# Layer 1's first mean square by column quarters of TensorE instead of eight full-width products

## What is computed

```python
def _rmsnorm(x, g):
    xf = x.astype(F32)
    y = xf * lax.rsqrt(jnp.mean(xf * xf, axis=-1, keepdims=True) + NORM_EPS)
    return (y * g.astype(F32)).astype(x.dtype)
...
    hn = _rmsnorm(h, g_mix_pre) * valid[None, :, None].astype(h.dtype)
    u = (hn @ w_in).astype(F32)
```

## Time and profile before

| | us |
|---|---|
| median of three runs | 973.7 (973.14 to 974.08) |
| the profiled execution's own time | 972.89 |
| its span, first to last instruction | 970.5 |
| TensorE busy in the span | 958.7 |
| VectorE / ScalarE / GpSimd busy | 605.5 / 515.1 / 79.8 |
| mean granted clock of TensorE | 0.997 |

### The profile page before, as it was taken

One profiled execution on the slowest core, in us unless ns is written; L12 is line 12 of the kernel. 1 busy time (PEld: TensorE's weight loads), 2 busy tenths in 40 slices (PEclk: granted clock), 3 DMA queues, 4 the chain that ended last, 5 costly groups with the idle time before them and its releaser, 6 DMA issues.

```text
span 970.5 us, 18994 instructions
## 1 busy us (share of the span) xinstructions
PE 958.7 (99%) x7428; PEld 906.2 (93%) x7428; DVE 605.5 (62%) x933; ACT 515.1 (53%) x825; POOL 79.8 (8%) x72
## 2 busy tenths in 40 slices
PE   9999999999999999999999999999999999999998
PEld 7999988899989999999989998888999899999886
DVE  7776575367857655553467775753678566565543
ACT  6645654475375544444456447444854655454542
POOL 1000000000031222210100000000000322122000
PEclk9999999999999999999999999999999999999999
DMA  7874433446462655555545653344465545656652
GB/s 217 298 220 148 130 95 124 131 131 174 155 193 91 198 172 174 175 176 165 170 131 159 206 165 120 114 132 131 132 180 168 174 130 185 198 179 197 215 177 85
DMA packets 164299, 158.02 MB, mean 163 GB/s; under 512 B 9603, under 2 KB 157294, under 8 KB 163854
## 3 DMA queue, kind: packets, MB, share of 16 engines
q1 hardware_dynamic: 163118, 153.76, 51.4%
q10 hardware_dynamic: 928, 3.33, 0.9%
q0 software_dynamic: 192, 0.07, 0.0%
HBM read 154.98 MB, written 1.05 MB: 161 GB/s over the span
## 4 chain that ended last, share of the span: by engine, by line
PE 92%; DVE 3%; DMA 2%; ACT 2%; issue 1%; DVEq 0%; SPq 0%
PE banks L690 24%; PE banks L692 24%; PE banks L691 24%; PE banks L1081 2%; PE banks L1083 2%; PE banks L1082 2%; DMA raw<-in_ffn_w_up 1%; PE banks L740 1%; PE banks L725 1%; DMA raw<-in_w_out 1%; PE banks L722 1%; PE banks L721 1%; PE banks L670 1%; DVE lo L1564 1%; PE banks L948 1%; PE banks L946 1%
## 5 line engine op out<-in xcount | busy, mean ns | idle before, releaser
L1564 DVE TENSOR_TENSOR lo<-raw,hi 128x1024 fp32r<-128x1024 f32 (+1 forms) x287 | 348.3, 1217 | 145.5 <-ACT hi L1165 145.3
L690 PE MATMUL banks<-xh,hi 128*128 128x272 f32 (+1 forms) x1456 | 420.6, 289 | 0.1
L692 PE MATMUL banks<-xh,lo 128*128 128x272 f32 (+1 forms) x1456 | 416.2, 286 | 0.0
L691 PE MATMUL banks<-xl,hi 128*128 128x272 f32 (+1 forms) x1456 | 415.1, 285 | 0.0
L1165 ACT ACTIVATE hi<-raw 128x1024 fp32r<-128x1024 f32 (+1 forms) x287 | 300.2, 1048 | 135.4 <-PE banks L692 45.4
L690 PEld LDWEIGHTS banks<-xh,hi 128*128 128x128 f32 x1456 | 274.3, 188 | 6.0 <-issue 4.2
L692 PEld LDWEIGHTS banks<-xh,lo 128*128 128x128 f32 x1456 | 274.5, 189 | 0.0
L691 PEld LDWEIGHTS banks<-xl,hi 128*128 128x128 f32 x1456 | 274.2, 188 | 0.0
L1269 ACT ACTIVATE gates<-banks,par 128x272 f32<-128x272 f32 (+1 forms) x64 | 30.7, 480 | 98.4 <-PE banks L692 92.4
L2058 POOL TENSOR_TENSOR silu_g<-silu_g,rstd 128x272 f32<-128x272 f32 (+1 forms) x44 | 54.6, 1240 | 219.0 <-ACT silu_g L1444 219.0
L2051 POOL TENSOR_TENSOR sq<-sq 128x272 f32<-128x272 f32 (+1 forms) x18 | 21.4, 1191 | 600.2 <-ACT sq L1429 599.4
(11 more groups left out here) (291 smaller groups left out, 1445.9 us busy)
## 6 DMA issues: line engine op xcount, KB each, us to landing
raw<-in_w_in SPq DMA_DIRECT2D x54, 1024.0 KB, 5.2
raw<-in_ffn_w_gate SPq DMA_DIRECT2D x22, 1024.0 KB, 5.2
raw<-in_ffn_w_up SPq DMA_DIRECT2D x22, 1024.0 KB, 5.3
raw<-in_ffn_w_down SPq DMA_DIRECT2D x19, 1024.0 KB, 5.1
raw<-in_w_out SPq DMA_DIRECT2D x8, 1024.0 KB, 5.3
raw<-in_w_in SPq DMA_DIRECT2D x12, 512.0 KB, 4.2
raw<-in_w_branch SPq DMA_DIRECT2D x12, 512.0 KB, 5.4
raw<-in_ffn_w_down SPq DMA_DIRECT2D x4, 768.0 KB, 4.3
```

The source lines that it names most:

```text
L690: mm(dst, wh, mh, start=start, stop=False)
L691: mm(dst, wh, ml, start=False, stop=False)
L692: return mm(dst, wl, mh, start=False, stop=stop)
L1564: tt(half_of(lo, g, c), half_of(raw, g, c), half_of(hi, g, c).bitcast(F32), ALU.subtract).then_inc(lo_ready, 2 if g in G_MIX else 1)
```

## The change

In layer 1's entry the eight full-width matmuls of the mean square go. In their place:

- `quarter_sums`: eight matmuls by `denind` (32 columns, the first all ones, the others zero), in two rounds of four. In a round the four matmuls write the four 32-partition quarters of bank 5, from `sq` tiles 0 to 3 in the first round and 4 to 7, accumulated, in the second. The first round stands inside the three tiles' run behind step k = 5, the second behind its end. Rows 0, 32, 64 and 96 then hold four partial sums, the other rows zero.
- `take_quarters`: a new ScalarE copy of that bank into `sq[:, 0]`, in front of the half of weights and of `root`.
- `mean_of_quarters`: one full-width fp32 matmul by `mean`, inside the first tile of mqk1, behind its step k = 4. It adds the four rows up and spreads the mean over all partitions.

```diff
+        if l:
+            stage("part0"), free(NORM_BANK)
         stage("norm0"), free(NORM_BANK)
...
-            def features(t, g, c, mh, ml, q0, i=0, step=0):
+            def features(t, g, c, mh, ml, q0, i=0, step=0, beside=None):
...
+                    if k == KT // 2 and beside:
+                        beside()
                 close_tile(last, t)
...
+            def quarter_sums(l, n, q0):
+                t = TILE[l][f"part{n}"]
+                ps = open_tile(t)
+
+                def four(at):
+                    pe.wait_ge(sq_ready[l][n], at + 4)
+                    for g in range(4):
+                        last = mm(ps[quad[g], 0:T - q0], cut["denind"], sq[:, at + g, q0:], start=at == 0, stop=at == 4)
+                    if at == 4:
+                        close_tile(last, t)
+                return four
+
+            def mean_of_quarters(l, n, q0):
+                wait_taken(pe, TILE[l][f"part{n}"])
+                t = TILE[l][f"norm{n}"]
+                close_tile(mm(open_tile(t)[:, 0:T - q0], cut["mean"], sq[:, 0, q0:], start=True, stop=True), t)
...
+                    four = quarter_sums(l, 0, 0)
                     together([(t, g, 0), (t + 1, g + 1, 0), (t + 2, g + 1, 1)], in_step(FIRST_LAGS[l]), uh, ul, 0, *ready,
-                             mean_square(l, 0, 0))
+                             lambda k: four(0) if k == 5 else None)
+                    four(4)
...
-                    features(t + j, g, j, mh, ml, group_start(l, name))
+                    features(t + j, g, j, mh, ml, group_start(l, name),
+                             beside=(lambda: mean_of_quarters(l, 0, 0)) if l and name == "mqk1" and j == 0 else None)
...
+            def take_quarters(l, n, q0):
+                t = TILE[l][f"part{n}"]
+                wait_tile(act, t)
+                taken(fn(sq[:, 0, q0:], bank_of(t)[:, 0:T - q0], ACT.Copy), t)
...
                         if k == 2:
                             round_half(half)
+                    take_quarters(l, 0, 0)
                     round_half(half + 1)
                     root(l, 0, 0)
```

## The result

The changed kernel takes **977.0 us** (median of 5 runs, 974.92 to 978.63) against 973.6 (5 runs, 973.02 to 974.08): 1.004 times the time before, 95% interval 1.0024 to 1.0055. Slower, inside the range of 974.0 to 977.9, and 1.3 us over the predicted 975.7. The profiled execution took 977.01 (before 972.89), its span is 974.6 (before 970.5): 4.1 us more.

What follows compares the result with a forecast made beforehand. TensorE was taken to bound the kernel, busy 958.7 of 970.5 us. The profiled 972.89 plus a 2.04 shift at gr's second tile gave 974.93; the median lies 0.81 above, so 975.7 us, range 974.0 to 977.9.

Steps and rivals of the forecast that it cites:

- The saving in the entry: Layer 1's entry on TensorE: 1.66 us less work, mqk1 opens 0.61 us earlier, the gate and gr's second tile 0.15 earlier.
- Where `rstd` goes: ScalarE and VectorE behind the entry: small read 2.85 us later, gwork's bank free at 524.73, gr's second tile 2.04 later.
- The covers: Entry and mqk1: the new copy, the half of weights, its load and the bias of small arrive in time, costing nothing.
- The shift stays 2.04 to the end: Behind gr's second tile: every step waits on a TensorE tile, so the 2.04 us delay lasts to the end.
- The clock falls: Rival, chance 0.33: the new wait at gr, or the entry's wider wait, lowers the clock; 1.68 us lost, total 977.4.
- The old fall is avoided: Rival, chance 0.08: the clock's fall in layer 1's output norm does not recur; 1.68 us come back, total 974.1.
- No wait at gr: Rival, chance 0.07: the gate's read-out is under 0.5 us later, so only the 0.15 saving remains, total 973.5.
- four one after the other: Rival, chance 0.03: each round's four matmuls in the entry run serially, 2.16 us instead of 0.78, total 978.5.

Runs made afterwards that it cites:

- r5: The changed kernel itself, timed again in 12 runs beside the follow-up kernels: 975.66 us, ratio 1.0025 to the kernel before.
- r1: The kernel before with only its eighth mean-square matmul moved into mqk1's first tile, behind step k = 4; no quarters, no copy: 976.39 us, ratio 1.0022.
- r2: The changed kernel with the spreading matmul behind step k = 1 of mqk1's first tile instead of k = 4: 975.13 us, ratio 1.0015.
- r11: The kernel before with gwork read out on ScalarE in front of the two halves of weights, rstd on time: 972.89 us, ratio 1.0005.
- r6: The changed kernel with the spreading matmul directly behind the second round, in front of mqk1: 976.13 us, ratio 1.0028.
- r9: r6 plus three full-width matmuls with discarded results at k = 0, 1, 2 of the entry: 974.52 us, ratio 1.0014.
- r4: The changed kernel plus three full-width matmuls with discarded results at k = 0, 1, 2 of the entry: 976.59 us, ratio 1.0022.

## Why the prediction was right, and where it wasn't

**The saving in the entry** (0.15 at the gate): 0.03 in r5's profile (20.36 for 20.39). mqk1 opens at 514.84 - 2.02 = 512.82, predicted 512.80, and a round takes what the head sums said: 0.60 to the next matmul and that one 0.32 in the chain instead of 0.12, together 0.80 for 0.78, and not the 0.46 alone that the 4x of the Trainium skill (TensorEngine Tiling (Array Packing), Theoretical Speedup) would leave. But part of the way out of the round is paid behind mqk1's first product (515.06 - 514.84 = 0.22 to the next start, not 0.12), so "mqk1 opens" looks 0.1 better than it is, and the gate is 0.12 late.

**Where `rstd` goes**: right within 0.05 us from Ln to the end of `gwork`, as shown above, Ln itself by two misses that cancel. TensorE goes on 0.10 later than predicted, 0.14 instead of 0.06 behind the end of the read-out. So the shift at the second tile of gr is 524.89 - 522.75 = 2.14, predicted 2.04, and the recorded wait 2.01, where 2.19 less 0.16 were predicted. r1 shows the cause by itself, r2 that the wait moves with Exp.

**The covers**: the copy, the half and the bias of `small` held. None appears in the waits.

**"The shift stays 2.04 to the end"**: right to the output norm (2.19), and wrong there. I had argued that every step waits on a tile of TensorE's. The wait in the output norm is for a load. The chain of waits before, and in r5:

```profile
761.98 6.75 DMA raw<-in_ffn_w_up
...
769.80 0.28 ACT sq L1429
770.08 0.04 issue
770.12 0.70 PE banks L740 x2
...
774.70 0.43 PE banks L740 x2
```

```profile
765.88 5.37 DMA raw<-in_ffn_w_up
...
772.33 0.28 ACT sq L1463
772.61 0.04 issue
772.65 0.71 PE banks L744 x2
...
776.87 0.43 PE banks L744 x2
```

The last squares stand on ScalarE behind a half whose load takes 6.75 us in the one and 5.37 in the other. Over the thirteen profiles the wait follows the load's time, whatever the kernel: 5.16 us gives 0.2 us of wait, 5.25 gives 0.4, 5.34 to 5.37 give 0.4 to 0.6 (five profiles), 5.74 gives 0.9, 6.01 gives 1.1, 6.49 gives 1.8, 6.55 and 6.70 give 1.9, and 6.75 gives 2.2. So the earlier trace rows showed me one value of something that spans 2 us, and a sum made against one profiled execution carries that value. Whether it is chance is only partly shown: the two profiles of the changed kernel have 6.49 and 5.37, but both profiles with `rstd` on time, before and r11, have long loads (6.75 and 6.55), and of the eleven others eight have less than 5.8. A later TensorE may itself shorten the load; no run tested that.

**The rivals.** *The clock falls*: this is what makes the first profile. Its fall is not in the new wait but in the entry's wider idle, 1.35 us in front of the third product of step 2, which the rival named as the other place. Its price was wrong. The gate comes 21.29 - 20.36 = 0.93 later than in r5, not 1.7, since TensorE waits for VectorE in the rest of the entry anyway and half the loss falls into those waits; r6 against r9 gives 1.01 for a fall at the same place. The falls come by chance: the same kernel had none there in r5. *The old fall is avoided*: the place is right, the first profile has a clock of 1.00 there, and the price is wrong. From the second mean matmul to the third take 774.70 - 770.12 = 4.58 with the fall, 4.22 (r5) and 4.21 (first profile) without. What runs slower there is filler (L670) and what would otherwise be waiting for ScalarE: 0.37 us, not 1.68. *No wait at gr* and *four one after the other* fell.

**The closing sum.** r5's span is 2.2 over before's: 2.02 for the later start of layer 1, 2.19 to the output norm, 5.12 - 7.17 = -2.05 within it, together 2.16. The first profile's is 4.1 over: 1.64 for the start, 3.12 to the output norm (2.19 and the fall), 6.41 - 7.17 = -0.76 within it, together 4.00. Neither total shows the 2.1 us of the change by itself; the marks do. Counted from layer 1's first product to the end of the span, before takes 471.4 us, and r5 and r1 take 471.6: in these two profiles the shorter load has given nearly all of it back. The first measurement lies 3.4 us over before. Beyond the 2.1 that leaves 1.3, which I put down to the clock: those five executions lost 4.2 thousandths of it, the next twelve 2.75, before's 1.8. That part is argued from averages, not shown; by the line's 0.9 us for a thousandth the clock's part would be 2.1 and the rest 1.3.

**The chances.** 0.62 for slower by over 0.2% came true, and the forecast's 975.7 was met by r5 and missed by 1.3 in the first measurement. That r5's profiled execution, 975.15, came so near the 974.93 that the sum gave for it is luck: two things that the sum left out cancel in it, layer 1 starting 2.02 later and the wait in the output norm being 1.7 shorter. A fall in the entry, for which the rival had 0.33, is seen in two of the five profiles of kernels with quarters and no fillers (the first, r6); its amount should have been 0.4 to 1.7, by place.

## What to carry to other kernels

Taking work out of a stretch in which the engine waits for another bought next to nothing here: 1.66 us of TensorE's work went and 0.03 came back. Ask what the moved result releases: an `rstd` 3.2 us later cost 2.0 us on a bank that only a queue on ScalarE frees, and changing that queue's order moved the loss to a late load. Before you take the price of a wait or a fall of the clock from one profile, see whether it is the engine's bound at that place, and whether a second profile has it at all.

## What was unexpected

- A weight load of 1 MB with the same place in the program took 5.16 to 6.75 us from profile to profile (6.49 and 5.37 in the two of the changed kernel), and TensorE's wait behind it 0.2 to 2.2 us.
- The granted clock fell behind waits of 0.8, 0.2 and 1.35 us in the entry (the first profile) and at a single wait of 2.0 us (r4), but not in r5 behind the same waits. One thousandth of the mean granted clock went with about 0.9 us of time (a straight line through the 224 executions with a level for each kernel).
- Four transfers issued by ScalarE took 2.45 us in ten profiles and 3.2 to 3.5 in three.
- GpSimd's addition of 128 x 272 holds up VectorE's by 0.5 us each time that they meet, and itself takes 0.91 to 0.96 in five of six cases here (1.73 in the sixth), where its group's mean before is 1.19.

What stays open: whether a wait of a given length brings the clock down can't be told from these profiles, since it fell and didn't fall behind the same one; what sets the load's landing time was not tried; and so it is open how much of the 2.1 us at gr an average execution still has at its end.
